# Encoder trunk in two mixer layers: two B-C products placed inside a projection unit, block transposes ahead of gating, head tables and first minima moved, unit 11's low part by adding transfer

## What is computed

```python
attn_out = window_attention(rope(q), rope(k), v, attn_sink)       # banded 128-query blocks
xbc = silu(depthwise_conv(xbc, ssd_conv_w, ssd_conv_b))           # width 5; split into xs, bm, cm
y = bidir_ssd(xs, dt_raw, dt_bias, a_log, bm, cm) + ssd_d * xs    # two directions, chunks of 128
#   in each chunk: y_diag = (cm @ bm^T * decay) @ (xs * dt), and a term from the other chunk
ssd_out = rms_norm(y * silu(z), ssd_norm_g)
h = layer_norm(ALPHA * h + concat(attn_out, ssd_out) @ w_out)
h = layer_norm(ALPHA * h + (silu(conv3(h @ w_gate)) * (h @ w_val)) @ w_down)
```

## Time and profile before

| | |
|---|---|
| runs (three) | 1298.28 us median, 1296.52 to 1298.59 |
| profiled execution | 1298.11 us, span 1296.3 us, mean granted clock 0.998 |
| busy: TensorE, DVE, ACT, POOL | 1280.9, 801.7, 609.2, 131.0 us |
| ACT's negated copy (L622) | 38 times, 1060 ns mean |
| POOL's issue of an adding transfer (L574) | 38 times, 868 ns mean |
| adding transfer, 512 KB, issue to landing | 5.5 us median |
| ACT, layer 0, high part of unit 11 | 62.52 to 63.57 us |
| ACT, then a table load of 1.28 us, and unit 7's tanh (L755) | starts at 66.00 us |

### The profile page before, as it was taken

The page is one execution under the profiler, slowest core; times in us unless marked ns, Lnnn a source line. Parts: engine busy times, 40 slices in busy tenths (PEclk is TensorE's granted clock), DMA queues, the critical chain, the costliest instruction groups (busy, mean ns, idle before and its releaser), DMA issues.

```text
span 1296.3 us, 17993 instructions
## 1 busy us (share of the span) xinstructions
PE 1280.9 (99%) x7456; PEld 1059.5 (82%) x7456; DVE 801.7 (62%) x1071; ACT 609.2 (47%) x913; POOL 131.0 (10%) x125
## 2 busy tenths in 40 slices
PE   9999999999999999999999999999999999999997
PEld 8877778889888888888898777788888888888886
DVE  7888898866444444342378998979654444443425
ACT  5766766436333333311276776653553333332112
POOL 2034511001000000000020354000100000000000
PEclk9999999999999999999999999999999999999999
DMA  5465565423333333323134656563133323223222
GB/s 200 158 147 115 132 146 138 172 77 103 98 98 98 98 98 98 130 98 97 54 127 150 151 114 150 129 179 130 66 114 98 98 98 96 96 93 129 96 95 111
DMA packets 43872, 151.36 MB, mean 117 GB/s; under 512 B 4912, under 2 KB 9424, under 8 KB 42640
## 3 DMA queue, kind: packets, MB, share of 16 engines
q1 hardware_dynamic: 38160, 130.01, 30.2%
q0 software_dynamic: 5632, 20.21, 9.1%
HBM read 141.81 MB, written 6.29 MB: 114 GB/s over the span
## 4 chain that ended last, share of the span: by engine, by line
PE 92%; DVE 6%; ACT 1%; issue 1%; DMA 0%; POOL 0%; SPq 0%; DVEq 0%
PE ps L870 17%; PE ps L871 17%; PE ps L872 17%; PE ps L1028 9%; PE ps L1029 9%; PE ps L1030 9%; PE ps L917 5%; PE ps L1242 2%; DVE cv L1476 2%; PE ps L896 1%; PE ps L1020 1%; DVE ast L1624 1%; PE ps L1189 1%; PE ps L1255 1%; PE ps L1226 1%
## 5 line engine op out<-in xcount | busy, mean ns | idle before, releaser
L870 PE MATMUL ps<-hhi,whi 128*128 128x512 f32 x1040 | 411.2, 395 | 0.9 <-DVE cv L1476 0.7
L871 PE MATMUL ps<-hlo,whi 128*128 128x512 f32 x1040 | 405.5, 390 | 0.0
L872 PE MATMUL ps<-hhi,wlo 128*128 128x512 f32 x1040 | 405.2, 390 | 0.0
L619 ACT ACTIVATE whi<-raw 128x1024 fp32r<-128x1024 f32 x208 | 219.4, 1057 | 214.6 <-DMA raw<-in_units 214.6
L1313 DVE TENSOR_TENSOR wlo<-raw,whi 128x1024 fp32r<-128x1024 f32 x170 | 207.8, 1224 | 149.4 <-ACT whi L619 149.4
L870 PEld LDWEIGHTS ps<-hhi,whi 128*128 128x128 f32 x1040 | 195.4, 188 | 49.3 <-issue 6.7
L872 PEld LDWEIGHTS ps<-hhi,wlo 128*128 128x128 f32 x1040 | 195.5, 188 | 41.3
L871 PEld LDWEIGHTS ps<-hlo,whi 128*128 128x128 f32 x1040 | 195.6, 188 | 39.4
L1028 PE MATMUL ps<-whi,uhi 128*128 128x512 f32 x352 | 137.1, 390 | 0.0
L1030 PE MATMUL ps<-wlo,uhi 128*128 128x512 f32 x352 | 137.0, 389 | 0.0
L1029 PE MATMUL ps<-whi,ulo 128*128 128x512 f32 x352 | 136.9, 389 | 0.0
(11 more groups left out here) (182 smaller groups left out, 1548.7 us busy)
## 6 DMA issues: line engine op xcount, KB each, us to landing
raw<-in_units SPq DMA_DIRECT2D x208, 512.0 KB, 3.5
wlo<-in_units POOLq DMA_DIRECT2D x38, 512.0 KB, 5.5
gb<-in_gb SPq DMA_DIRECT2D x5, 1024.0 KB, 5.5
h_kept<-hb SPq DMA_DIRECT2D x2, 2048.0 KB, 8.9
ha<-h_kept SPq DMA_DIRECT2D x2, 2048.0 KB, 9.6
hb<-in_x SPq DMA_DIRECT2D x4, 512.0 KB, 5.8
v_rep<-v_tm SPq DMA_DIRECT2D x32, 64.0 KB, 2.1
out_y<-hb SPq DMA_DIRECT2D x8, 256.0 KB, 2.0
```

Of the source, the lines that this page charges most:

```text
L619: A(whi[:, m % RING, :], raw[:, m % RING, :], ACT.Copy).then_inc(unit_hi, 1)
L870: mm(out, whi[:, slot, cols], xhi, start=start, stop=False)
L871: mm(out, whi[:, slot, cols], xlo, start=False, stop=False)
L872: return mm(out, wlo[:, slot, cols], xhi, start=False, stop=stop)
```

## The change

Five edits: unit 11 joins the units of the adding transfer; CB 0 and CB 2 are done by TensorE in the middle of units 13 and 15 (between the fourth and the fifth tile), and stand, for ACT's evacuation, behind the exponentials AX of units 12 and 14; PT stands ahead of SIL2 and XS in units 9 to 15; the head tables MV 0 to 3, which were written at the ends of units 15, 16, 17 and 17, are written in unit 15 (0 and 1) and unit 16 (2 and 3, ahead of XS); and SB 0 and SC 0 stand right behind SILU of unit 17, ahead of its SIL2.

```diff
-BY_DMA = range(12, 31)
+BY_DMA = range(11, 31)
+CB_AT = {13: 0, 15: 2}
@@ mixer_schedule
-        if n in (13, 15):
+        if n in CB_AT:
             steps += [("CB", n - 12)]
         if 4 <= j < N_CONV:
             steps += [("T", j)]
-        if n in (12, 14):
-            steps += [("CB", n - 12)]
@@
             steps += [("AX", i)]
+        if n + 1 in CB_AT:
+            steps += [("CB", CB_AT[n + 1])]
         steps += [("SH" if n >= U_CONV else "S", n + AHEAD)]
@@
         if 1 <= i < 8:
-            steps += [("SIL2", n - 1 - U_CONV)]
+            steps += [("PT", i - 1), ("SIL2", n - 1 - U_CONV)]
             if n - 1 - U_CONV >= 4:
                 steps += [("XS", n - 1 - U_CONV)]
-            steps += [("PT", i - 1)]
+        if n == 15:
+            steps += [("MV", 0), ("MV", 1)]
@@
             steps += [("SILU", n - U_CONV)]
+            if n == 17:
+                steps += [("SB", 0), ("SC", 0)]
             if not 0 <= i < 8:
                 steps += [("SIL2", n - U_CONV)]
...
-            if n == 17:
+            if n == 16:
                 steps += [("MV", 2), ("MV", 3)]
             if n - U_CONV >= 4 and i >= 8:
                 steps += [("XS", n - U_CONV)]
...
-        if 15 <= n < 17:
-            steps += [("MV", n - 15)]
-        if n == 17:
-            steps += [("SB", 0), ("SC", 0)]
-        elif a >= 0:
+        if a >= 0:
@@ tensor
+            def mixed(L, i):
+                pe.wait_ge(silu_done, L * N_CONV + 4)
+                wait_aux_free(pe, L, ("CB", i))
+                for g in range(2):
+                    last = mm(ps[:, aux_bank(("CB", i)), g * SEQ:(g + 1) * SEQ], bc[:, g, i * BLK:(i + 1) * BLK],
+                              bc[:, 2 + g, i // 2 * SEQ:(i // 2 + 1) * SEQ], start=True, stop=True)
+                last.then_inc(aux_full, 1)
@@ "G"
-                        between = functools.partial(values, L, AV_AT[i]) if i in AV_AT else None
+                        between = None
+                        if i in AV_AT:
+                            between = functools.partial(values, L, AV_AT[i])
+                        elif i in CB_AT:
+                            between = functools.partial(mixed, L, CB_AT[i])
                         by_columns(unit(L, i) % RING, unit_bank(i), between)
@@ "CB"
-                    elif what == "CB":
...
+                    elif what == "CB" and i not in CB_AT.values():
+                        mixed(L, i)
```

## The result

The changed kernel is slower: 1303.45 us median (1297.57 to 1307.76, 20 runs) beside 1298.31 (1296.45 to 1301.29, 20 runs) of the kernel before; ratio 1.0034, 95% interval 1.0023 to 1.0046. The prediction was 1292.3 and faster. The profiled execution took 1305.11 us with a span of 1303.3, 7.0 us more than before.

The account below looks back on a forecast made before the run. TensorE, 99% busy, was taken as the bound, so only its waits could be won: 3.65 us in layer 0 plus 2.26 in layer 1, together 5.9, gave 1292.3 us; own range 1290.6 to 1293.5, with (a), (b), (c) 1290.4 to 1295.0.

Parts of the forecast that it names:

- the one on the tables: Head tables moved on POOL to units 15 and 16, beside gatings 8 and 9: cost 0, up to 1 us.
- Case (c): Moved tables block gatings 8 and 9 and so `alo` 3: 1 us lost per layer, 1294.3 us; chance 0.05.
- the scores of block 4: On TensorE: to start at 96.58, from the added transfer and earlier transposes together, 0.4 us gained per layer.
- the product inside unit 13: CB 0 mid-unit, 0.9 us long: 7.85 us between scores of blocks 4 and 5, gaining 3.15 and 1.46 us.
- T4: First x transpose on TensorE, awaiting unit 11's gating: a new wait of 0 to 1.2 us, 0.3 taken per layer.
- the first off-block product: TensorE's wait there for the minimum goes because the minimum runs before gating 10: 0.6 and 0.9 us gained.
- rival (e): ACT, in order, stands at its evacuation until TensorE is half through units 13 and 15: slower, 1300.0 us; chance 0.05.
- Gatings behind the transpose: DVE, units 9 to 12: gating meets only the tail of POOL's normalization, gaining 0 to 0.4 us per step, 0.2 taken.
- The sum of 3.65 and 2.26 us: Forecast gains of layer 0 and layer 1 over all terms, together 5.9 us.
- The 3.15 us of layer 0: Gain forecast from CB 0 inside unit 13: 11.00 us between scores of blocks 4 and 5 becomes 7.85.
- Rival (b): Layer 0's low clock near 100 us comes even without the stall: 1.14 us back, 1293.4 us; chance 0.10.

Follow-up runs that it names:

- products_only: Kernel before with only the B-C products CB 0 and CB 2 moved inside units 13 and 15: 1297.99 us, ratio 0.9982.
- transfer_only: Kernel before with only unit 11 by adding transfer: 1298.47 us, ratio 0.9997.
- minima_only: Kernel before with only the first own-decay product and first minima ahead of gating 10: 1298.05 us, ratio 0.9986.
- tables_behind_x: Changed kernel with head tables 2 and 3 written behind x product 9 in unit 16, not ahead of it: 1292.93 us, ratio 0.9959.
- tables_only: Kernel before with only head tables 0 to 3 placed as in the change: 1303.74 us, ratio 1.0036.
- transposes_only: Kernel before with only the block transposes ahead of gating: 1298.63 us, ratio 1.0000.
- halves: Changed kernel with each head table written by two GpSimd instructions of half the size, at the same places: 1296.91 us, ratio 0.9980.
- table_x_table: Changed kernel with x product 9 between head tables 2 and 3: 1298.75 us, ratio 0.9996.

## Why the prediction was wrong

**The step that failed** is the one on the tables: "They now fall beside gatings 8 and 9, whose slack is 1 us; 0 taken, up to 1 for the range." Case (c) had the mechanism, the place and a price of 1 us per layer. The price was too small by a factor of 3 to 4. I let the gating wait for one table; it waited for both, 3.3 us more than its 0.69 against a slack of 1, so T8 waited 2.45 and 2.70. And I gave the new stall no half clock, after having read in the earlier trace rows what one costs. Together that made 4.16 us in layer 0 and 4.41 in layer 1 of the profile, 5.9 to 6.7 for both layers in the medians. I dismissed the case on a slack of 1 us that I compared with a table of 2, though the order of POOL's steps placed both tables where gating 9 comes. The trace of before had shown more of this already. There gating 8, beside table 0, takes 1.50 us near 138, so "gatings of 1.5 us and more near 138" was no sign of (c); the sign came at T8 and not at L1215:

```profile
137.18 1.50 DVE L1483 SCALAR_TENSOR_TENSOR xsc<-xsc,cv 128x512 f32<-128x512 f32 x1
```

**The stall that no step had.** The 2.73 us in the values, with 1.8 for the clock, were neither in the sum nor in a rival. That an engine's instructions come by the same DMA engines as its data was to be seen in the page's queue table, but nothing in the trace of before waited for them. Its cause is shown as far as this: in three kernels without unit 16's adding transfer the stall falls to 0.2 to 0.4 us, and the upper group of times goes in both that had one. When TensorE asks for the packet, no record tells; that it queues behind the transfer is read from the starts of packets, not measured in the queue. For it speaks that in seven of the eight profiles with the stall the packet starts in the last 0.1 to 0.5 us of the transfer (products_only: 2.3 us before its end). The kernel before may be subject to it too: transfer_only and minima_only, which change little, had it in their profiles. Its times lie near 1296.5, 1298.4 and 1300.2, but which of them had this stall no profile shows; its one profile had none.

**The steps that held.** In layer 0 the scores of block 4 came 0.43 us earlier (0.4 taken); the product inside unit 13: 7.64 us to the next scores (7.85 forecast), 0.68 for the product (0.9); T4 waited 0.47 and 0.46 (0.3 taken, 0 to 1.2 bounded); the first off-block product no longer waited; ACT never made TensorE wait, rival (e) falls. Gatings behind the transpose took 0.95 for 1.11, the 0.2 taken. The sum of 3.65 and 2.26 us stands beside 3.80 and 2.37 in tables_behind_x, against the same profile of before. The times agree less plainly. The median of tables_behind_x, 1292.93, is near the forecast 1292.3, but beside runs of before at 1300.05 and with two of six times at 1296.6 and 1296.8; by the ratio, 0.9959, it is 5.3 us faster, for 5.9.

**A term that was partly luck.** The 3.15 us of layer 0 hold some 1.65 us of half clock (11.00 less 9.35 below), taken from one execution. From the scores of block 4 to those of block 5 the profile of before takes 11.00 us; four other profiles with the same stall at CB 0 (transfer_only, minima_only, tables_only, transposes_only) kept 2.4 GHz there and take 9.38, 9.35, 9.33 and 9.11, as layer 1 does. How many runs of the kernel before had it, no record tells, so in the medians this term may be worth much less. Rival (b), a low clock near 100 us in any case, finds nothing in its favour: none of the nine profiles without the stall at CB 0 has it there.

**The lock rule** of the Trainium skill (SBUF — State Buffer, Who interferes with whom) was the rule that spoke against the change. It says that the second comer waits for the whole instruction of the first; gating 8 (1.84, and 0.99 with halves) and table_x_table's gating 9 (2.15) agree: each ends 0.54 to 0.57 us behind the GpSimd instruction that ran when it came. The 3.99 us beside two tables in a row don't: that gating ends 0.55 us behind the second, so it did not get its turn between them. Gating 8, also beside two in a row, did, and the second table took 2.35 us for 1.90. Both came 0.6 us behind the start of a table. One difference is to be seen: gating 8 stands directly behind another DVE instruction, gating 9 comes after 0.70 us of idle. No run changed that, so what decides is open.

## What to carry to other kernels

A step moved on an engine that "has time" is to be checked against what the other engine does at its new place, instruction by instruction: 4 us of GpSimd work that nobody waited for made VectorE wait 3.3 us, and TensorE behind it stand 2.5 us and lose its clock. Look at both neighbours before giving such a move a zero; the place of two tables was worth 5.9 to 6.7 us here. A clock loss seen in one execution is not a sure gain: put it into the range, not into the sum. Where the times of a kernel fall into groups, profile both: here a 16 KB packet of instructions beside a 512 KB transfer parted groups 3 to 6 us from each other, and the upper one vanished with that transfer.

## What the runs showed of the hardware

- A DVE instruction with two SBUF inputs (0.69 us alone) took 3.99 to 4.00 us beside two GpSimd multiplies in a row, 4.06 us together (three profiles, both layers), 2.15 beside one, and 1.84 where it came in beside the first of two at another place.
- TensorE's instructions come in packets of 16 KB, mostly 0.9 to 1.4 us each, 59 for 14912 matmuls and weight loads. In eight profiles the packet that starts at 112.2 to 113.2 us, within unit 16's adding transfer, goes with a stall of 1.6 to 3.2 us, always in the values of block 1; in the six profiles where one started by 110.2 the stall there was 0 to 0.4.
- In the mixers half clock came with eleven stalls of TensorE of 1.7 to 3.2 us, and lasted 3.4 us, or 6.8 in two profiles. Thirteen others of 1.4 to 2.4 us kept 2.4 GHz, those of 1.9 and 2.4 in tables_only among them.
